# Halved first projections and a later wait for the state stores in a two-layer hybrid step

## The reference

```python
sh1, sc1, gt1, sh2, sc2, gt2 = split(silu(cond) @ w_mod[l] + b_mod[l], 6)
h = rmsnorm(x, g_mix[l]) * (1 + sc1) + sh1
aq, ak, av, mq, mk, mv, mo, mi, mf = split(h @ w_in[l])   # 512 128 128 512 512 512 512 8 8
att = attention(rope(norm(aq)), rope(norm(ak)), av)       # 8 heads of 64, cached keys for latents
h_ml, final_state = mlstm_both_ways(mq, mk, mv, mi, mf)   # 4 heads of 128, running maximum
x = x + gt1 * (concat(att, sigmoid(mo) * norm(h_ml)) @ w_out[l])
h = rmsnorm(x, g_ffn[l]) * (1 + sc2) + sh2
x = x + gt2 * grouped_top2_experts(h)                     # 16 experts, 1024 x 512, SwiGLU
```

## Time and profile before

| | |
|---|---|
| median of 3 runs | 802.85 us (802.13 to 803.07) |
| profiled execution | 801.58 us, its span 799.8 us |
| PE busy | 758.4 us (95%) |
| DVE busy | 329.3 us (41%) |
| ACT busy, POOL busy | 158.2 us, 56.6 us |
| moved by DMA | 289.41 MB, mean 362 GB/s |
| chain that ended last | PE 77%, DMA 14%, SyncE's queue 3%, DVE 2% |

### The profile page before, as it was taken

How to read it: one execution, slowest core, us unless ns; L and a number is a source line. 1 busy time by engine, 2 the same in 40 slices (tenths; PEclk the granted TensorE clock), 3 DMA queues, 4 the chain that set the end, 5 groups by cost and what they waited for, 6 DMA issues and landing times.

```text
span 799.8 us, 10907 instructions
## 1 busy us (share of the span) xinstructions
PE 758.4 (95%) x4676; PEld 402.2 (50%) x4683; DVE 329.3 (41%) x534; ACT 158.2 (20%) x355; POOL 56.6 (7%) x69
## 2 busy tenths in 40 slices
PE   3799999989999999999889999999999999999997
PEld 2364547866534433444244746688653443344423
DVE  0379567614323232123218974782332223212323
ACT  2202125402312012020003111261131201202001
POOL 0040060101100000000000003300010000000000
PEclk9999999999999999999999999999999999999999
DMA  8999809998999999999999780479889999999993
GB/s 348 398 380 378 356 7 379 407 376 315 429 420 424 424 421 424 427 418 424 421 405 409 290 346 0 163 287 398 343 312 403 427 424 421 424 426 418 424 421 157
DMA packets 49857, 289.41 MB, mean 362 GB/s; under 512 B 3400, under 2 KB 5760, under 8 KB 23696
## 3 DMA queue, kind: packets, MB, share of 16 engines
q1 hardware_dynamic: 48080, 285.30, 88.0%
q0 software_dynamic: 1488, 3.31, 1.2%
q10 hardware_dynamic: 240, 0.08, 0.0%
HBM read 286.31 MB, written 2.37 MB: 361 GB/s over the span
## 4 chain that ended last, share of the span: by engine, by line
PE 77%; DMA 14%; SPq 3%; DVE 2%; issue 2%; ACT 1%; POOL 0%; DVEq 0%; ACTq 0%
PE ps L1100 23%; PE ps L764 14%; PE ps L1130 12%; PE ps L1014 6%; DMA ring<-in_w_e_up 5%; PE ps L1084 4%; DMA ring<-in_w_e_down 4%; DMA ring<-in_w_in 3%; PE ps L639 3%; PE ps L1145 2%; PE ps L778 2%; SPq L544 1%; DMA ring<-in_x_sample 1%; DMA out_new_state_n<-nst 1%; SPq L584 1%
## 5 line engine op out<-in xcount | busy, mean ns | idle before, releaser
L1100 PE MATMUL ps<-ring,xe 128*64 128x512 f32 x688 | 151.6, 594 | 3.7 <-DMA ring<-in_w_e_up 3.7
L764 PE MATMUL ps<-ring,hT 128*128 128x512 f32 (+1 forms) x320 | 125.3, 551 | 2.4 <-DMA ring<-in_w_in 2.4
L1100 PEld LDWEIGHTS ps<-ring,xe 128*64 128x64 f32 x688 | 48.6, 137 | 104.7 <-issue 99.6
L764 PEld LDWEIGHTS ps<-ring,hT 128*128 128x128 f32 x320 | 60.2, 190 | 64.1 <-issue 58.4
L1130 PE MATMUL ps<-ring,ex 128*32 128x512 f32 x736 | 92.2, 594 | 0.2 <-issue 0.2
L1992 DVE COPY ye<-ps 64x512 f32<-64x512 f32 (+1 forms) x28 | 19.3, 689 | 164.2 <-PE ps L1130 164.0
L1014 PE MATMUL ps<-hT,ring 128*128 128x256 f32 x256 | 58.8, 389 | 0.0
L1976 DVE RECIPROCAL ex<-ex 128x512 f32<-128x512 f32 x16 | 53.6, 3353 | 0.6
L1014 PEld LDWEIGHTS ps<-hT,ring 128*128 128x128 f32 x256 | 49.1, 194 | 7.8 <-issue 0.8
L1130 PEld LDWEIGHTS ps<-ring,ex 128*32 128x32 f32 x736 | 26.0, 110 | 52.3 <-issue 49.4
L1974 DVE TENSOR_SCALAR ex<-ex 128x512 f32<-128x512 f32 x16 | 6.8, 427 | 109.4 <-ACT ex L1526 109.4
(11 more groups left out here) (272 smaller groups left out, 805.2 us busy)
## 6 DMA issues: line engine op xcount, KB each, us to landing
ring<-in_w_mod SPq DMA_DIRECT2D x24, 2048.0 KB, 19.5
ring<-in_w_e_up SPq DMA_DIRECT2D x23, 2048.0 KB, 19.7
ring<-in_w_e_gate SPq DMA_DIRECT2D x20, 2048.0 KB, 22.8
ring<-in_w_e_down SPq DMA_DIRECT2D x19, 2048.0 KB, 23.0
ring<-in_w_in SPq DMA_DIRECT2D x10, 2048.0 KB, 23.4
beside<-in_w_e_gate SPq DMA_DIRECT2D x8, 2048.0 KB, 25.5
beside<-in_w_e_down SPq DMA_DIRECT2D x7, 2048.0 KB, 19.6
beside<-in_w_e_up SPq DMA_DIRECT2D x5, 2048.0 KB, 17.9
```

The lines of the kernel that those rows point to most:

```text
L764: mm = pe.matmul(bank[:, 0:width], hT[:, k, b * P:(b + 1) * P], w[:, k, :], start=(k == 0), stop=(k == KD - 1))
L1100: mm = pe.matmul(bank[PLACES * j:PLACES * j + PLACES, :], xe[:, k, c:c + PLACES], w[:, j, i, :], start=(k == 0), stop=(k == KD - 1))
```

## The change

Layer 0 alone gets another beginning. Section (0, 0) is cut into two halves of the features: section (0, -1) makes shift and scale for the first four contraction chunks of `hT`, (0, 0) for the last four. Each has two blocks, of all 8 contraction rows by 512 columns, and rows of its own (`feature_rows`). mk, mq and mv are loaded in two halves of the contraction; the first halves are issued between the two sections, the second halves behind them. The first halves raise `front_in`, the second ones `slot_landed`. TensorE multiplies the first halves, with the second section's rows and columns in between, then the second halves. mq's banks are cleared with a product of zeros first, and mv moves to banks 4 and 5. Section (0, 1)'s blocks stand behind akv and behind mo, and VectorE's turns take one, two and one block, not three and one. The tokens are issued ahead of all blocks and transposed first. VectorE's and ScalarE's wait for `state_out` moves from the mixing to the start of the next layer.

```diff
+SECTION_CHUNKS[0, -1], SECTION_CHUNKS[0, 0] = (0, 8), (4, 8)
+HALVED = ("mk", "mq", "mv")
-BETWEEN = {"mk": (0,), "mq": (1, 2), "mv": (3,)}
-SUM_TURNS = (((0, 1, 2), (3,), ()), ((0, 1, 2), (3,), ()))
+BETWEEN = ({"akv": (0, 1), "mo": (2, 3)}, {"mk": (0,), "mq": (1, 2), "mv": (3,)})
+SUM_TURNS = (((0,), (1, 2), (3,)), ((0, 1, 2), (3,), ()))
...
-        put(("gates", l), 4)
+        put(("gates", l), 6 if l == 0 else 4)
         for g in PROJ:
             for b in range(NB):
-                turn((g, b))
-        put(("gateT", l), 5)
+                if l == 0 and g == "mv":
+                    put((("mv", b), 0), 4 + b)
+                else:
+                    turn((g, b))
+        put(("gateT", l), 7 if l == 0 else 5)
...
-            load_section(0, 0, 0)
             sp.dma_start(cst[:, 0:P], t["constants"][:, 0:P]).then_inc(const_in, 16)
             for b, name in enumerate(("x_prompt", "x_sample")):
                 sp.dma_start(xtok[:, b, :], t[name][0]).then_inc(x_in, 16)
-            load_section(0, 0, 1, 2, 3)
...
+            load_features(-1)
+            for g, landed in zip(HALVED, front_in):
+                if weights[g, 0][0] == RING - 1:
+                    taken(sp, ("x", 0), ("x", 1), ("x", 2), ("x", 3))
+                load_rows(g, slice(0, KD // 2), landed)
+            load_features(0)
+            for g in HALVED:
+                load_rows(g, slice(KD // 2, KD), slot_landed[weights[g, 0][0]])
...
-                project("mk", fresh=True)
-                project_turned("mq", (0,))
-                gates()
-                project_turned("mq", (1,))
-                gate_rows()
-                project("mv")
+                if l == 0:
+                    front, back = range(0, KD // 2), range(KD // 2, KD)
+                    project("mk", fresh=True, ks=front)
+                    project_turned("mq", range(NB), front)
+                    feature_rows(0, 0, 1)
+                    project("mv", (0,), ks=front)
+                    section_columns(0, 0)
+                    project("mv", (1,), ks=front)
+                    project("mk", fresh=True, ks=back)
+                    project_turned("mq", (0,), back)
+                    gates()
+                    project_turned("mq", (1,), back)
+                    gate_rows()
+                    project("mv", ks=back)
...
-                act.wait_ge(state_out, 16 * STATE_OUTS * (l + 1))
                 squares_mid(l)
...
             for l in range(DEPTH):
+                if l > 0:
+                    dve.wait_ge(state_out, 16 * STATE_OUTS * l)
                 normalise(l)
...
-                dve.wait_ge(mod_ready, 2 * l + 2)
-                dve.wait_ge(state_out, 16 * STATE_OUTS * (l + 1))
+                dve.wait_ge(mod_ready, 2 * l + 3)
```

More of the change, by code:

```diff
@@ L148, in bank_plan @@
         put(("x", r), r)
-    put(("modrow", 0, 0), 7)
-    put(("modcol", 0, 0), 7)
+    for s in (-1, 0):
+        put(("modrow", 0, s), 7)
+        put(("modcol", 0, s), 7)
     for l in range(DEPTH):
@@ L248, in put @@
         order.append(slot)
-    for i in range(section_slots(0, 0)):
-        put(("mod", 0, 0, i))
+    for s in (-1, 0):
+        for i in range(section_slots(0, s)):
+            put(("mod", 0, s, i))
+    for g in HALVED:
+        put((g, 0))
     for l in range(DEPTH):
         for g in PROJ:
-            put((g, l))
-            for i in BETWEEN.get(g, ()):
+            if l > 0 or g not in HALVED:
+                put((g, l))
+            for i in BETWEEN[l].get(g, ()):
                 put(("mod", l, 1, i))
@@ L408, in build @@
         first_read, last_half = sem("first_read"), sem("last_half")
+        front_in = [sem(f"{g}_front_in") for g in HALVED]
         sum_step = sem("sum_step")
@@ L644, in section_rows, with feature_rows @@
                         done(("modrow", l, s), mm)
+            def feature_rows(s, *which):
+                bank = begin(("modrow", 0, s)) if 0 in which else ps[banks["modrow", 0, s][0]]
+                for v in which:
+                    w = landed(("mod", 0, s, v)).rearrange("p (k n) -> p k n", k=KD)
+                    for k in range(KD):
+                        for g in range(4):
+                            mm = pe.matmul(bank[32 * g:32 * g + 32, v * P:(v + 1) * P], cT[:, NB * k:NB * k + 32],
+                                           w[:, k, g * P:(g + 1) * P], start=(k == 0), stop=(k == KD - 1))
+                    if v == 0:
+                        mm.then_inc(mod_read, 1)
+                    else:
+                        done(("modrow", 0, s), mm)
             def section_columns(l, s):
@@ L706, in raw_logits @@
                             done((("logits", b), l), mm)
+            pe.wait_ge(ones_set, 3)
+            warm(("x", 0), 12)
             pe.wait_ge(const_in, 16)
[L709 to L713, removed]
             pe.wait_ge(x_in, 16 * NB)
@@ L721, in _ @@
                 done(("x", r), mm)
+            pe.wait_ge(rows_in, 16 * ROW_LOADS * DEPTH)
+            for l in range(DEPTH):
+                bank = begin(("rows", l))
+                done(("rows", l), pe.transpose(bank[:, 0:ROWS_L], rowsin[:, l, :], ident[0:ROWS_L, 0:ROWS_L]))
             def section_sums(l, s):
@@ L767, in project, with project_turned @@
                                 norm_total(l, 1)
-                        done(((g, b), l), mm)
-                def project_turned(g, which):
-                    w = landed((g, l)).rearrange("p (k n) -> p k n", k=KD)
+                        if ks[-1] == KD - 1:
+                            done(((g, b), l), mm)
+                def project_turned(g, which, ks=range(KD)):
+                    w = block_of(g, ks).rearrange("p (k n) -> p k n", k=KD)
                     for i in which:
-                        bank = begin(((g, i), l))
+                        bank = begin(((g, i), l)) if ks[0] == 0 else ps[banks[(g, i), l][0]]
+                        if ks[0] == 0 and len(ks) < KD:
+                            pe.matmul(bank[:, :], zeros[:, :].broadcast_to([P, P]), zeros[:, :].broadcast_to([P, 512]), start=True,
+                                      stop=False, skip_group_check=True)
                         for j in range(2):
                             h = 2 * i + j
-                            for k in range(KD):
+                            for k in ks:
                                 mm = pe.matmul(bank[:, j * TOK:(j + 1) * TOK], w[:, k, h * MD:(h + 1) * MD], hT[:, k, :],
-                                               start=(k == 0), stop=(k == KD - 1))
-                        done(((g, i), l), mm)
+                                               start=(k == 0 and len(ks) == KD), stop=(k == KD - 1),
+                                               skip_group_check=len(ks) < KD)
+                        if ks[-1] == KD - 1:
+                            done(((g, i), l), mm)
                 def gates():
@@ L1361, in _ @@
                     root_in(l, 1)
[L1362 to L1365, removed]
+                    for s in (-1, 0):
+                        section_row(0, s)
+                        act.wait_ge(mod_ready, s + 2)
+                        for b in range(NB):
+                            act.wait_ge(xr_ready, 2 + b)
+                            modulate(0, 0, sq, b, (4 * s + 4, 4 * s + 6))
+                else:
+                    act.wait_ge(mod_ready, 2 * l + 2)
+                    modulate_in(0)
                     part_in(l, 1)
                     root_in(l, 1)
-                modulate_in(1)
+                    modulate_in(1)
                 for b in range(NB):
```

83 lines of the change are left out of this document (58 added, 25 removed).

## The result

The changed kernel takes 809.23 us (median of 4 runs, 808.31 to 809.88), the kernel before, timed beside it, 802.49 (801.36 to 803.07). The ratio is 1.0079, with a 95% interval from 1.0058 to 1.01: slower by 6.7 us. The forecast was 810.0 in a range from 799 to 815. The profiled execution took 809.01 us, with a span of 807.1 beside 799.8 before: +7.3.

The account below looks back on a forecast made before the run. Bound: the load stream, set by how early each layer's mixer frees ring slots; layer 0's mixer runs on TensorE. +10.7 +1.8 -5.3 = +7.2 us on 801.58 gives 808.8, the median 1.27 above: 810.0, range 799 to 815.

Parts of the forecast that it names:

- The late copy: VectorE's copy of scanT in layer 0, for which TensorE's max_rows waits: at 103.6 and not 92.88, +10.7 us.
- the chain of small loads: GpSimd's loads in layer 0: 36.1 us from mk's landing to the start of VectorE's scans, brt landing at 76.7.
- The clock: TensorE after 17 us of idle in front of max_rows, layer 0: lower granted clock, 1.8 us charged once.
- The state wait: Layer 0's mixing: without the wait for the state stores TensorE goes straight on to the raw logits, -5.3 us.
- That the small loads aren't late: Rival, layer 0: their chain shortens or mk's half lands faster, scanT copied at 96.8, +0.4 us, 803.3; chance 0.12.
- That the halves pay in full: Rival: TensorE isn't held at max_rows, layer 0's mixer ends 6 to 10 us earlier, 788 to 791; chance 0.08.
- the point of decision that I named: At max_rows, layer 0: a scanT copy made by 87, 16.6 us before the predicted date, leaves TensorE unheld.
- That the mixing gives nothing back: Rival: the stream, not TensorE, sets layer 0 behind the state wait, all 12.5 us remain, 815.4; chance 0.10.
- mk's start: First mk matmul in layer 0: near 22 to 23 and not 33.73, its first half needing two w_mod blocks.

Follow-up runs that it names:

- 64 dead products: Kernel before with only the state waits moved, plus 64 one-column products of zeros at the start of TensorE's program: 794.15 us, ratio 0.9887.

## Why the prediction came out

**The late copy** is the mechanism, link by link. Predicted and measured: mk's second half 40.7 and 41.37, brt 76.7 and 78.7, scan_columns 86.3 and 87.67, the copy 103.6 and 105.43. The missing 1.8 us are 0.7 of the landing of mk and 1.3 of the chain of small loads, which I had left at its old length, less 0.1 in the sums. Term: +10.7, measured +12.55. The edit that puts the copy first removes the idle and its clock price, so the link is shown and not argued.

**The clock** was mis-sized: 1.8 us charged, 3.15 measured. I took the price from one idle, of 3.50 us. A longer idle isn't simply dearer, though. By the same count (max_rows and mo against 2.00 and 20.91 us) the price was 3.15 us after an idle of 17.41, 4.21 after 11.62 and 3.03 after 2.76; in the mixing it was 1.7 after 3.50 and nothing after 2.77. What sets it is open.

**The state wait** as a term was right to 0.1 us for the two traces compared (15.7 - 5.3 = 10.4), and the kernel before gains 5 by this edit alone. It isn't what the edit is worth in the changed kernel, where putting the waits back costs nothing that can be told (0.5 us by the medians, 0.2 in the mixing of the traces). I held the stores' landing fixed to the mixer. It is not: the mixing came 15.7 us later and the landing 11.5, with GpSimd's stand in front of the stores at 5.81 us for 10.47. So most of these 5.3 us would have come back without the edit.

**The rest of the sum.** These three terms, as measured, make +10.4 and not the forecast +7.2. That the median still lay 0.8 us from the forecast was luck, and due to a term that I didn't have: the stand at the branch, 5.3 us, which the kernel before has and the changed one has not, less 1.8 us at the end of layer 1, which I left at nothing and whose cause was not tested. The size of the forecast was thus met by two errors against each other. Without the difference in position the change costs 9 to 13 us.

**The rivals.** That the small loads aren't late: they were, and setting them off earlier in fact gives 803.5, near the 803.3 that this rival was given, but with the copy at 99.3 and not 96.8 and no stand at the branch, so that this nearness is partly chance. That the halves pay in full: they don't even with the copy first (805.5), since the sums then hold the akv copies; the point of decision that I named, a copy by 87, was nearly met there at 87.8, and the time was 14 us above that rival's upper figure. There was a second bound on VectorE behind the first that I hadn't priced. That the mixing gives nothing back: no idle, and 5.3 recovered. mk's start at 25.61 missed the 22 to 23 by 3 us, which was hidden in the idle. The rows of the second w_mod block began only at 19.90 and took 3.45 us, at a clock granted at 0.50 from 21 to 23.

## What to carry to other kernels

Before work is put ahead on one engine, find the first product of another engine that it will wait for, and ask what sets that product's date: here a semaphore whose event moved later and sums placed ahead of one 0.22 us copy turned 4.5 us gained at scan_columns into 15.7 lost at the end of mo. A gain shown by removing a wait in one kernel is not a property of the edit; test it in the kernel that it ends up in: the state wait gave 5 us in the kernel before, 2 with 64 dead products, and none in the changed kernel. And when a few us are at stake, compare kernels whose code lies alike, or shift both by some dead instructions, before a difference is put down to the change.

## What the runs showed of the hardware

- The same instructions of TensorE behind a branch cost 5.2 us more or less in the traces with the number of instructions ahead of them: a stand of 3.5 us with 0 and 128 dead products, none with 64 and 192, in the changed kernel the other way round (none with 0, 3.70 us with 64). That the code is fetched anew at the branch was not shown; the rows say "issue" alone.
- After 17.41 us of idle, TensorE's clock was granted at 0.50 until 112, that is for over 6 us of work; the first 16 matmuls took 3.78 us for 2.00. After idles of 11.62 and 2.76 us they took 3.78 as well.
- Blocks of 2 MB in runs of 2 KB arrived at 387 GB/s, in runs of 8 KB at 416 to 429 (one execution each).
- From GpSimd's last issue of a state store to its landing it was 8.7 us in the kernel before (162.04 to 170.78) and 8.6 with the waits put back (175.21 to 183.86); what varied was GpSimd's own stand in front of the issue, 10.47 and 7.17 us. The cause of that is open.
